# Retention in a hybrid encoder layer: the last projection units of a head placed inside the head itself

## The reference

```
scores = einsum('blhd,bmhd->bhlm', q, k) * decay
inner  = einsum('bhlm,bmhe->blhe', scores, v)
cross  = einsum('blhd,bhde->blhe', q * q_decay, state)
new_state = exp(lg * L) * state + einsum('blhd,blhe->bhde', k * k_decay, v)
y = inner + cross        # then a group norm over the head's 256 values
```

## Time and profile before

| | us |
|---|---|
| median of 3 runs | 2204.34 (2202.94 to 2204.92) |
| the profiled execution, its own time | 2203.62 |
| its span, first to last instruction | 2201.7 |
| PE busy | 2062.5 (94%) |
| DVE busy | 1086.7 (49%) |
| ACT busy | 662.3 (30%) |
| POOL busy | 348.9 (16%) |

### The profile page before, as it was taken

The page is one execution under the profiler, slowest core; times in us unless marked ns, Lnnn a source line. Parts: engine busy times, 40 slices in busy tenths (PEclk is TensorE's granted clock), DMA queues, the critical chain, the costliest instruction groups (busy, mean ns, idle before and its releaser), DMA issues. The chain is left out here.

```text
span 2201.7 us, 33255 instructions
## 1 busy us (share of the span) xinstructions
PE 2062.5 (94%) x13370; PEld 1979.3 (90%) x13370; DVE 1086.7 (49%) x1820; ACT 662.3 (30%) x1191; POOL 348.9 (16%) x307
## 2 busy tenths in 40 slices
PE   7879898987998988999999999988999999999997
PEld 6768787876998887999999999988999999999997
DVE  7966767764444433321111224475555556432257
ACT  4434444441112223321121113354434334310010
POOL 2110000000122111000000000144444444300000
PEclk9989999998999999999999999999999999999998
DMA  3511110115111112221124112423233232473412
GB/s 146 217 45 41 40 45 31 45 35 212 59 33 59 41 42 72 82 67 42 48 91 158 38 48 79 132 76 119 90 109 115 85 118 98 165 297 137 165 58 82
DMA packets 88842, 201.60 MB, mean 92 GB/s; under 512 B 11664, under 2 KB 42320, under 8 KB 85904
## 3 DMA queue, kind: packets, MB, share of 16 engines
q1 hardware_dynamic: 88720, 199.89, 26.3%
HBM read 141.71 MB, written 58.15 MB: 91 GB/s over the span
## 5 line engine op out<-in xcount | busy, mean ns | idle before, releaser
L800 PE MATMUL ps<-xn_hi,w_hi 128*128 128x384 f32 (+1 forms) x960 | 320.6, 334 | 20.4 <-DMA xn_lo<-xn_spill 12.6
L800 PE MATMUL ps<-sx_hi,t_hi 128*128 128x272 f32 x1056 | 306.3, 290 | 12.1 <-ACT u L1495 5.9
L802 PE MATMUL ps<-xn_lo,w_hi 128*128 128x384 f32 (+1 forms) x960 | 317.5, 331 | 0.0
L801 PE MATMUL ps<-xn_hi,w_lo 128*128 128x384 f32 (+1 forms) x960 | 317.5, 331 | 0.0
L801 PE MATMUL ps<-sx_hi,t_lo 128*128 128x272 f32 x1056 | 306.0, 290 | 0.0
L802 PE MATMUL ps<-sx_lo,t_hi 128*128 128x272 f32 x1056 | 304.8, 289 | 0.0
L800 PEld LDWEIGHTS ps<-sx_hi,t_hi 128*128 128x128 f32 x1056 | 200.8, 190 | 13.1 <-issue 6.9
L800 PEld LDWEIGHTS ps<-xn_hi,w_hi 128*128 128x128 f32 x960 | 183.9, 192 | 24.5 <-DMA xn_lo<-xn_spill 15.7
L801 PEld LDWEIGHTS ps<-sx_hi,t_lo 128*128 128x128 f32 x1056 | 200.5, 190 | 0.1
L802 PEld LDWEIGHTS ps<-sx_lo,t_hi 128*128 128x128 f32 x1056 | 200.5, 190 | 0.0
L801 PEld LDWEIGHTS ps<-xn_hi,w_lo 128*128 128x128 f32 x960 | 183.9, 192 | 0.0
(11 more groups left out here) (245 smaller groups left out, 4757.3 us busy)
## 6 DMA issues: line engine op xcount, KB each, us to landing
w_stage<-in_weights SPq DMA_DIRECT2D x83, 512.0 KB, 3.7
y_spill<-hg_r SPq DMA_DIRECT2D x44, 544.0 KB, 3.3
yd<-y_spill SPq DMA_DIRECT2D x22, 1088.0 KB, 5.6
raw<-in_weights SPq DMA_DIRECT2D x22, 512.0 KB, 5.1
hg<-in_weights SPq DMA_DIRECT2D x22, 512.0 KB, 5.1
d_stage<-in_weights SPq DMA_DIRECT2D x24, 384.0 KB, 3.1
ym_spill<-out_hl SPq DMA_DIRECT2D x32, 256.0 KB, 2.6
xt<-in_x SPq DMA_DIRECT2D x8, 544.0 KB, 8.1
```

Of the source, the lines that this page charges most:

```text
L800: nc.tensor.matmul(out, wh, xh, start=start, stop=False, skip_group_check=onto)
L801: nc.tensor.matmul(out, wl, xh, start=False, stop=False, skip_group_check=onto)
L802: return nc.tensor.matmul(out, wh, xl, start=False, stop=stop, skip_group_check=onto)
```

## The change

It changes where the units stand, not their order. `RET_CUT` says how many units of a head run in the head before it: all 15 of head 0 (in the attention), 12 of head 1, 9 of head 2, 7 of head 3. The rest run inside the head itself. A head carries its own rest first and then the next head's first ones: 12, 12, 13 and 8 units. There is one ahead of each B; a second behind N of the first `twice` chunks (1, 1, 2 and 0) and behind N of chunk 8; what is left stands ahead of Z of chunk 8, which now is the last step. PE waits for V of the own chunk in B, in place of the wait for V8 ahead of the first A.

```diff
+RET_CUT = (15, 12, 9, 7)
 def retention_steps(head):
-    fill = [("R", head + 1, *unit) for unit in RET_UNITS] if head + 1 < RH else []
+    fill = [("R", head, *unit) for unit in RET_UNITS[RET_CUT[head]:]]
+    fill += [("R", head + 1, *unit) for unit in RET_UNITS[:RET_CUT[head + 1]]] if head + 1 < RH else []
+    twice = max(0, len(fill) - 11)
     steps = [("A", 0)]
     for c in range(9):
         if fill:
...
         steps.append(("N", c))
-        if fill:
+        if fill and (c < twice or c == 8):
             steps.append(("F", *fill.pop(0)))
         if c:
             steps.append(("Z", c - 1))
-    steps.append(("Z", 8))
-    return steps + [("F", *unit) for unit in fill]
+    steps += [("F", *unit) for unit in fill]
+    return steps + [("Z", 8)]
...
                             pe.wait_ge(rot_sum, 1 + rot_index["R", h, "K", NG - 1])
-                            pe.wait_ge(p_free, 1 + p_order["R", h, "V", 8])
...
                         pe.wait_ge(sc_mid, n + 1)
+                        pe.wait_ge(p_free, 1 + p_order["R", h, "V", c])
                         out = ps[0:L, 1, 0:DV]
```

## The result

The changed kernel takes 2177.22 us (median of 4 runs, 2175.56 to 2177.66) against 2203.72 us (median of 4 runs, 2202.94 to 2204.92), a ratio of 0.9878 (95% interval 0.9861 to 0.9895). The forecast was 2170.7 us, and 33.3 us were forecast where 26.5 came. The kernel became faster, as forecast, and the time lies within 2167 to 2179; but that is the range with rival 1 in it, and the forecast's own range, 2167 to 2173, was missed by 4 us.

A forecast was written before the change was run, and what follows sets the result against it. PE paces the retention, so only its waits and half-clock time can be won. 11.0 + 18.8 + 6.1 - 1.7 - 0.9 = 33.3 us saved gave 2170.7 us, range 2167 to 2173, or to 2179 with rival 1.

The forecast's parts named there:

- rival 1: The clock falls at the four short pauses of PE too: 5.5 to 8 us lost, about 2177 us, chance 0.12.
- (f): Queues of VectorE, GpSimd and SyncE, and the moved wait for V: units cover each chunk's chain, at no cost.
- Rivals 2 and 3: One unit doesn't cover a chunk's chain: 2192 us, chance 0.04; queues lock into step with PE: 2227 us, chance 0.02.
- (a): Last head: V1 to V8 ahead of its B steps fill the waits for `st_f`, saving 11.0 us.
- (b): Ends of heads 0 to 2: units fill the waits, saving 15.1 us, plus 3.7 of slow clock, 18.8 in sum.
- (c): Last K unit to first V unit, heads 0 and 1: shorter pause saves 3.1 us, kept clock 3.0, sum 6.1.
- (d): V8 to the next head's Q0, heads 1 and 2: a new wait of about 0.85 us each, costing 1.7.
- (e): End of the last head: V8 with its cast and `w_lo` ahead of B of chunk 7 costs 0.9 us.

The follow-up runs named there:

- e1: The change with heads 0 and 1 as before it, head 2 carrying 7 units of head 3, the last head its V1 to V8: 2197.1 us, ratio 0.9968.
- e3: The change with step Z of the chunk before moved from behind A to ahead of B: 2176.1 us.
- e9: The kernel before the change with only the wait for V moved and no unit moved: 2204.1 us, ratio 1.0005.
- e5: The change with two units in the last head's chunk 0, so V8 stands ahead of B of chunk 6: 2176.0 us.
- e7: The change with the cast of the gate loop's first weights behind zt of chunk 6 and `w_lo` behind zn of chunk 7: 2177.1 us.
- e2: The change with every head still carrying all 15 units of the next, rearranged at the heads' ends, none in the last head: 2196.5 us, ratio 0.9961.
- e4: The change with a third double chunk in head 2, so K2 stands ahead of B of chunk 8: 2175.3 us.
- e6: The change with head 2's chunks 0, 1 and 4 doubled: K2 earlier, V8 and Q0 kept apart: 2173.0 us, ratio 0.9859.

## Why the prediction was right, and 6 us too good

- **(f), the cover, held.** This is the step on which the sign hung. One unit between two chunks hides the state, the mask and `zn` completely: no wait between 783 and 819, and none for these three in heads 0 to 2. Rivals 2 and 3 fell with it, and e1 shows it apart from the rest.
- **(a)** forecast 11.0, measured 24.27 - 13.73 = 10.5 us. The 0.5 is A at 0.33.
- **(b)** forecast 15.1 for the ends, measured 3 x (7.01 - 3.0) = 12.0: the term that was most wrong. I priced chunk 8 like a full chunk, while the rows of before had its own price in view: A with 64 rows took 0.46, and B 1.75 us of which I took 0.45 for waiting. These two make 0.7 of the 1.0 us a head; the rest is Z of chunk 8 and the V units beside it. The 3.7 us of slow clock behind the ends came in full: A and the first unit of heads 1 and 2 now take 0.31 and 2.96 us.
- **Not in the sum**: with one unit a chunk, A stands directly ahead of Z in 17 chunks of heads 0 to 2 where a unit stood between them before; 17 x 0.08 = 1.4 us. (A unit behind a step of the chunk has such 0.08 us in its own price, see the last section, and the number of units is the same.) The last head of before had A at 0.33 in the same order, so this too could be read. e3 shows that the order can't remove it.
- **(c)** forecast 6.1, measured 3.4 of pauses and 2.8 of clock, less 0.2 because head 2's V0 took 4.53 instead of 4.37: 6.0 us. **(d)** forecast 1.7, measured 2 x 0.90 = 1.8.
- **(e)** forecast 0.9, measured 8.91 - 7.06 = 1.85: the wait was as derived, but for the 0.11 us of the moved wait, which (f) had at 0 (e9), and on top of it the clock fell before B of chunk 8 had ended (2.54 us against 1.75). e5 and e7 show that V8's cast and `w_lo` are the cause of the wait, by moving them: 7.18 and 7.33 us.

The sum by measured terms: 10.5 + 12.0 + 3.7 - 1.4 + 6.0 - 1.8 - 1.85 = 27.2 us, against 27.5 in the stretch. The missing 5.8 us are hence, within 0.3, PE's own small steps (3.1 + 1.4 + 0.5) and the end of the last head (0.95: 0.8 of clock, 0.1 of the moved wait), no wait in a new place.

**Rival 1** did not happen: at the four short pauses the clock stayed at 1.00. Its number, about 2177 us, is nevertheless the one that was measured. That is luck: the steps that were priced too low cost as much as the fall of the clock would have, and the time lies in the stated range only because the range was widened for that rival. The total alone would have pointed to the wrong cause; the clock in the windows and the units' times tell them apart. The Trainium skill's page "TensorE: Matmul & The Clock Gate", in the section "A second HAM failure mode: psum-queue depth-cycling", says that frequent short idles make the clock swing. The traces here don't show it: four pauses of 0.9 to 1.3 us in 190 us left it at 1.00, and so did the closer pauses of 0.8 us in the last head before. The rival's price was real, though: e2 and e4 brought it about with pauses of 2.05 and 2.5 us.

Two small slips of the prediction: with (d) at 0 and (c) covered its range would begin at 2170.7 - 4.5 = 2166.2, not 2167; and "no chunk now has just one" unit leaves out chunk 0 of heads 1 and 2, which have Q0 alone. Neither bears on the result.

## What to carry to other kernels

Spreading independent work evenly over a dependent chain is worth what the uncovered links lose, and one unit a link was enough here, though it took twice as many links to place it; what remains to be priced are the junctions, since a step of 64 rows or a short matmul ahead of another costs more than its share of a full one, and a wait put behind the one at which an engine stands costs something even when it is long met. When units are moved, ask for each pair that shares a buffer (here K2 and V0, V8 and Q0) what now stands between them: e4 won 3.3 us at one pair and lost nearly all at the other, and e6 kept it by choosing another chunk. What an engine does behind a unit, such as a weight cast, moves with the unit and should not land ahead of the chain's own steps at an end that nothing covers.

## What the runs showed of the hardware

- Pauses of PE of 0.9 to 1.3 us between stretches of full work left the granted clock at 1.00 in every case; pauses of 2.05 us (e2, twice) and 2.5 us (e4) were followed by 1.2 GHz (a mean of 0.79 over 8 us), and Q units of 4.27 us became 5.8. The wait of 1.58 us ahead of B of the last head's chunk 8 went either way: B took 2.54 us in the change, 1.75 in e1. A pause of 2.96 us was followed by 1.2 GHz in most cases, but in e9 once it was not: V0 behind a wait of 2.71 us took 2.95 us at a clock of 1.00. The cost of one and the same wait thus differs by 1.5 us between executions, and Q0 of a head took 5.22, 6.44 or 6.71 us behind nearly the same waits. I take this for a part of the scatter of 2 to 4 us between runs of one kernel, which was not tested.
- The change from A or Z to what follows costs 0.08 us. A (128 columns, 0.25 us) takes 0.33 when another step of the chunk follows, and with Z moved the 0.08 appeared at Z (e3). Where a unit follows, it is there too, inside the unit: a V unit behind A took 791.08 - 788.12 = 2.96 us and the V unit directly behind it 793.96 - 791.08 = 2.88 (e5). So the order of the steps can move it but not remove it, as e3 found. The cause was not looked for.

```profile
788.12 0.36 PE L804 MATMUL ps<-w_hi,xn_hi 128*128 128x256 f32 x1
...
791.08 0.28 PE L804 MATMUL ps<-w_hi,xn_hi 128*128 128x256 f32 x1
...
793.96 0.38 PE L1043 MATMUL ps<-s_prompt,rq 128*128 128x256 f32 x1
```

- Steps with 64 rows are not cheaper but dearer: B 1.75 to 1.77 us against 1.30, A 0.46 against 0.25 to 0.33.
- A wait on a semaphore that had long been met, placed behind the wait at which PE stands, delayed B by 0.11 us twelve times in e9 and in none of the B that found the mask ready. e2, which has the same wait, shows the same 2.99 us between uncovered chunks (832.50 - 829.51).
